# First stage of a fused two-block kernel: the inputs are loaded first, the modulation products run in four column groups with four weight buffers, and the first projection is issued by parts

## The chip, the core and the metric

The kernel is one program on one core of a Trainium2 chip. Its engines each follow their own instruction list and meet only at semaphores: TensorE (PE in the rows, PEld for its weight loads), VectorE (DVE), ScalarE (ACT), GpSimd (POOL) and SyncE (SP), which issues all DMAs of this kernel. The metric is the device time of one execution in microseconds, the median of several runs. Everything the kernel multiplies is float32. Large products are made from three cheaper ones: each operand is split in a rounded part (`_hi`) and a remainder (`_lo`), and hi·hi + hi·lo + lo·hi is accumulated. The small products of the first stage are plain float32 instead, and such a matmul shows in the trace as two records.

## What is computed

Two transformer-like blocks on 256 tokens of width 1024. The change touches only the beginning of the first:

```python
sh1x, sc1x, g1x, sh2x, sc2x, g2x = split(silu(c) @ w_ada + b_ada, 6)      # modulation for x
sh1c, sc1c, ...                  = split(silu(c_ctx) @ w_ada + b_ada, 6)  # and for the context
hc = rms_norm(ctx, norm1_g) * (1 + sc1c) + sh1c
hx = rms_norm(x,   norm1_g) * (1 + sc1x) + sh1x
z  = hx @ w_in      # u, vs, q, r, ga, gb, k, v, lr;  of hc only k, v, lr
```

After that come a spatial gating unit, a two-directional gated linear attention (GLA) with its log-decays from `lr`, a merge, a convolutional FFN, and then the whole second block (gated delta rule, two more FFNs).

## The kernel before

Activations stand transposed: 128 partitions by 8 slices `k` of the width, by tokens. `x` and `ctx` are normalized and modulated side by side, so a slice of `a_parts` (`a_hi`, `a_lo`) has 256 + 256 columns. Weights of the projections stream as units of 512 KB, 128 x 1024 each, through four slots of `w_raw`: SP loads unit u when GpSimd has split unit u-4 (`lo_ready`), ScalarE rounds it to `w_hi` (line 1622) once TensorE has used the slot, GpSimd subtracts to `w_lo` (line 644), TensorE multiplies. Units 0 to 3 are `w_k`, 4 to 7 `w_q`, 8 to 15 `w_v`, 16 to 23 `w_vs`.

The first stage, up to the `w_k` tiles:

- **Modulation rows.** The first 2048 columns of `w_ada` (shift and scale) are in four blocks j of 2 MB, in two buffers `adab`. `mod_rows(j)` on TensorE (line 1000) multiplies `silu(c)`, `silu(c_ctx)` as a stationary operand of 2 columns with 8 slices of 512 columns, into 2 partitions of bank 6 or 7. ScalarE copies them to `modrow`, `flip_rows(j)` (line 1011) transposes them back into columns.
- **Norm.** ScalarE squares each slice, VectorE adds slices 0 to 5 (`sum_squares`, line 2554), `mean_square` (line 1023) adds the rest over partitions on TensorE, ScalarE takes the root, VectorE the reciprocal.
- **Modulated operand.** For each j VectorE normalizes two slices of both inputs (lines 2587, 2588), builds `mod` and `gain`, and forms the full product and its remainder `a_lo` (lines 2601, 2528), ScalarE writes `a_hi`.
- **`w_k` tiles.** `tile_blocks(s, k0, k1)` (line 1033) multiplies slot s with slices k0 to k1; tiles 0 and 1 start with slices 0 to 3, the last two slices of all four tiles come at the end.
- Then `w_q` (line 734), the low-rank `lr` product (line 1061), and `w_v` by blocks (line 1090), which needs units 8 to 11 at once. Beside its second slices go eight small `logits` products (line 1072), each followed by an `Abs` on ScalarE and an add on VectorE, in two banks, so they pace each other.

The other four fifths of `w_ada` (g1, sh2, sc2, g2) are needed only for x and are not done on TensorE: 16 pairs of rows `p` of 1 MB each go through seven buffers (`adaw`, the table `ADA_RING`) and VectorE multiplies and sums them (`modulations`, line 2621, four instructions for each p). SP issues them by `ada_rows(p)` between the units. The order of every engine is written out by hand; a wait of SP holds up all later DMAs.

## Time and profile before

| | us |
|---|---|
| median of 3 runs | 1280.89 (1279.03 to 1281.66) |
| the profiled execution | 1280.58 |
| its span, first to last instruction | 1278.8 |
| around the span | 1.8 |
| TensorE busy in the span | 1248.2 (98%) |
| start of the `w_k` tiles / of `w_q` / of `w_v` on TensorE | 40.2 / 62.8 / 80.5 |
| squares of ctx / of x start on ScalarE (8 take 2.56) | 16.1 / 21.0 |
| mean granted TensorE clock | 0.990 |

The busy time of TensorE in the profile is pipelined: a record lasts from the issue of a matmul to its modelled end and overlaps the next. What an operation costs is read from start to start. Start times are from the span's start.

### The profile page before, as it was taken

The page shows a single profiled execution, that of the slowest core. Times are in us where ns is not written, and L with a number is a line of the kernel's source. Part 1 is how long each engine was busy: PE and PEld are TensorE (multiplying, and loading weights), DVE is VectorE, ACT ScalarE, POOL GpSimd, SP SyncE. Part 2 cuts the span into 40 slices and gives each one's busy share as a digit, 9 for nine tenths or more (in the row PEclk, how much of TensorE's full clock was granted, in tenths as well). Part 3 has the DMA queues.
Part 4 walks back from the last instruction along what each step waited for, and adds up shares of the span by engine and source line. Part 5 has one row for each costly group of instructions (what it writes and reads, how often), then busy time and mean ns, then how long its engine had stood idle before and what let it go on. Part 6 is the DMA issues. An engine that isn't in the chain of part 4 may idle for free.

```text
span 1278.8 us, 26332 instructions
## 1 busy us (share of the span) xinstructions
PE 1248.2 (98%) x9155; PEld 1161.0 (91%) x9155; DVE 726.7 (57%) x1674; ACT 710.6 (56%) x1283; POOL 881.5 (69%) x387
## 2 busy tenths in 40 slices
PE   9999999999999999999899999999999999999997
PEld 3688899999988898899799989999999999999986
DVE  3989861142487773276864256545633766555633
ACT  3656644553666665476532247656755556666743
POOL 0457957578869888965422237888788887888795
PEclk9999999999999999999989999999999999999999
DMA  9986255356646656734312115555566565665562
GB/s 368 403 340 197 83 199 165 118 162 183 184 137 205 192 178 173 211 109 118 113 51 83 51 55 177 181 174 180 155 186 187 174 181 161 187 182 180 157 194 76
DMA packets 66021, 217.71 MB, mean 170 GB/s; under 512 B 9897, under 2 KB 17321, under 8 KB 62609
## 3 DMA queue, kind: packets, MB, share of 16 engines
q1 hardware_dynamic: 65936, 216.56, 53.6%
q8 instruction: 57, 0.93, 0.3%
q14 instruction: 28, 0.22, 0.1%
HBM read 215.48 MB, written 1.05 MB: 169 GB/s over the span
## 4 chain that ended last, share of the span: by engine, by line
PE 51%; issue 24%; POOL 20%; ACT 2%; DVE 2%; POOLq 0%; ACTq 0%; DVEq 0%
POOL w_lo L644 20%; PE bank L734 13%; PE bank L757 10%; PE bank L849 6%; PE bank L1090 5%; PE bank L763 5%; PE bank L858 3%; PE bank L766 2%; PE bank L853 1%; PE bank L1179 1%; DVE cbuf L2934 1%; PE bank L1156 1%; ACT w_hi L1622 0%; PE bank L695 0%; PE bank L700 0%
## 5 line engine op out<-in xcount | busy, mean ns | idle before, releaser
L644 POOL TENSOR_TENSOR w_lo<-w_raw,w_hi 128x1024 fp32r<-128x1024 f32 x340 | 814.0, 2406 | 359.5 <-ACT w_hi L1622 358.6
L1622 ACT ACTIVATE w_hi<-w_raw 128x1024 fp32r<-128x1024 f32 (+1 forms) x372 | 377.9, 1020 | 126.0 <-PE bank L858 42.7
L757 PE MATMUL bank<-a_hi,w_hi 128*128 128x264 f32 (+3 forms) x704 | 200.5, 285 | 0.1
L757 PE MATMUL bank<-a_hi,w_lo 128*128 128x264 f32 (+3 forms) x704 | 200.2, 284 | 0.0
L757 PE MATMUL bank<-a_lo,w_hi 128*128 128x264 f32 (+3 forms) x704 | 199.9, 284 | 0.0
L734 PE MATMUL bank<-a_parts,w_hi 128*128 128x256 f32 x960 | 173.8, 284 | 0.2
L734 PEld LDWEIGHTS bank<-a_parts,w_hi 128*128 128x128 f32 x960 | 149.7, 192 | 1.0 <-ACTq L1879 0.5
L734 PE MATMUL bank<-a_parts,w_lo 128*128 128x256 f32 x480 | 135.8, 283 | 0.0
L757 PEld LDWEIGHTS bank<-a_hi,w_hi 128*128 128x128 f32 x704 | 132.8, 189 | 0.4 <-DVE a_lo L3515 0.3
L757 PEld LDWEIGHTS bank<-a_lo,w_hi 128*128 128x128 f32 x704 | 132.9, 189 | 0.1
L757 PEld LDWEIGHTS bank<-a_hi,w_lo 128*128 128x128 f32 x704 | 132.9, 189 | 0.0
L3589 DVE SCALAR_TENSOR_TENSOR bank<-row_mean,cols,bank 128x260 f32<-128x260 f32 (+3 forms) x112 | 54.6, 488 | 117.2 <-ACT cols L1622 112.8
L734 PEld LDWEIGHTS bank<-a_parts,w_lo 128*128 128x128 f32 x480 | 92.1, 192 | 0.0
L849 PE MATMUL bank<-g_parts,w_hi 128*128 128x512 f32 x308 | 79.1, 397 | 0.7 <-DVEq L3691 0.7
L2934 DVE SCALAR_TENSOR_TENSOR cbuf<-bank,pv,cbuf 128x189 f32<-128x189 f32 (+2 forms) x176 | 65.6, 423 | 16.4 <-ACT cbuf L1622 15.8
L651 POOL TENSOR_TENSOR w_lo<-w_raw,w_hi x32 | 58.0, 1842 | 24.0 <-ACT w_hi L1622 23.2
L734 PE MATMUL bank<-a_hi,w_hi 128*128 128x272 f32 (+1 forms) x240 | 73.6, 307 | 0.0
L734 PE MATMUL bank<-a_hi,w_lo 128*128 128x272 f32 (+1 forms) x240 | 71.6, 298 | 0.0
L734 PE MATMUL bank<-a_lo,w_hi 128*128 128x272 f32 (+1 forms) x240 | 71.5, 298 | 0.0
L763 PE MATMUL bank<-a_parts,w_hi 128*128 128x512 f32 x256 | 64.2, 393 | 1.7 <-DVE cbuf L2934 1.7
L849 PEld LDWEIGHTS bank<-g_parts,w_hi 128*128 128x128 f32 x308 | 55.0, 188 | 11.1 <-DVEq L3691 0.9
L886 PE MATMUL bank<-g_parts,w_hi 128*128 128x260 f32 x352 | 63.9, 284 | 0.7 <-DVEq L3691 0.7
(523 smaller groups left out, 2785.3 us busy)
## 6 DMA issues: line engine op xcount, KB each, us to landing
w_raw<-in_s SPq DMA_DIRECT2D x284, 512.0 KB, 3.6
w_raw<-in_down SPq DMA_DIRECT2D x48, 512.0 KB, 3.6
adaw<-in_w_ada SPq DMA_DIRECT2D x16, 1024.0 KB, 10.3
w_raw<-in_down SPq DMA_DIRECT2D x24, 384.0 KB, 3.2
adab<-in_w_ada_first SPq DMA_DIRECT2D x8, 1024.0 KB, 8.9
ctxt<-in_ctx SPq DMA_DIRECT2D x1, 1024.0 KB, 11.3
x<-in_x SPq DMA_DIRECT2D x1, 1024.0 KB, 15.3
out_h<-h SPq DMA_DIRECT2D x4, 256.0 KB, 2.6
```

What stands on the lines that cost most here:

```text
L644: pool.tensor_tensor(w_lo[:, s], w_raw[:, s], w_hi[:, s].bitcast(F32), ALU.subtract) \
L651: pool.tensor_tensor(w_lo[:, :, ds(k, 1)], w_raw[:, :, ds(k, 1)], w_hi[:, :, ds(k, 1)].bitcast(F32), ALU.subtract) \
L734: ins = mm(banks[s][:, first:n], w_[:, s, k], x_[:, k, first:n], start=(m == 0), stop=(m == 3 * KD - 1))
L757: ins = mm(banks[bank][:, tk], w_[:, s, k], x_[:, k, tk], start=(m == 0), stop=(m == 3 * KD - 1))
L763: mm(banks[bank][:, :].rearrange("p (two n) -> p two n", two=2), w_hi[:, s, k], a_parts[:, :, k, N1:], start=(k == 0), stop=False)
L849: mm(dst[:, :].rearrange("p (two n) -> p two n", two=2), w_hi[:, s, k], g_parts[:, :, kk, first:n], start=(kk == 0), stop=False)
L858: ins = mm(dst[:, 0:N1], w_lo[:, s, k], g_hi[:, kk, first:n], start=False, stop=(kk == KF - 1))
L886: ins = mm(banks[t][:, first:N2], w_[:, s, k], x_[:, k0 + k, first:N2], start=(m == 0), stop=(m == 3 * KF - 1))
L1090: ins = mm(banks[b][:, :].rearrange("p (u m) -> p u m", u=SLOTS), x_[:, k, tk], w_[:, :, k], start=(k == 0 and i == 0), stop=(k == KD - 1 ...
L1622: return nc.scalar.activation(out_, in_, f, **kw)
L2934: v.scalar_tensor_tensor(dst, frm(banks[banks_of(p)[0]][:, 0:n]), pv[:, ds(pair + w, 1)], dst, ALU.mult, ALU.add).then_inc(conv_seq, 1)
L3589: return v.scalar_tensor_tensor(dst, row_mean[:, N2 - dst.shape[-1]:], by, dst, ALU.mult, ALU.add)
```

## The change

- **SP** loads `ctx`, the constants and `x` first, then block 0 of `w_ada`, units 0 to 3, then blocks 1 and 2; block 3 waits only for the squares' buffers (`std_ready`). There are now four buffers `adab`, each in two halves, on the places of the later `adaw` buffers; `ADA_RING` is renumbered accordingly.
- **Norm sums** are made by TensorE alone: `mean_square` has 8 matmuls instead of 3, VectorE's `sum_squares` is gone. x has a bank of its own (5).
- **`mod_rows`**: the stationary operand is `c2_wide`, 32 columns of which 2 are not zero. Slice k goes to partitions 32·(k mod 4) onward, so four slices in a row use four different column groups, and the result is four partial sums. ScalarE copies all 128 partitions, and `flip_rows` is no transpose but a matmul with `row_pick` (128 x 2), which picks and adds the four partials.
- **Order on TensorE**: 24 instead of 16 warming matmuls, both norm sums, then `mod_rows(0)`; `fill` (dummy 128x128 matmuls, 5, 4 and 8) between; the first two slices of every `w_k` tile before `mod_rows(1)` to `(3)` or between them, and the rest by parts of two slices across all four tiles.
- **VectorE** normalizes all of `ctx` while the norm of x is still under way. Of the later rows it does 7, 1, 1, 6 where it did 9, 1, 1, 4 around the same three fixed steps (`w2s`, `lrs`, the log-decay adds).
- **ScalarE** rounds `w2` (`w2s`) after the copies of `w_q` instead of before them.

```diff
-            for j in range(4):
-                if j >= 2:
-                    sp.wait_ge(ada_done, j - 1)
...
+            small(ctxt[:], a["ctx"], ctx_in)
+            small(averages[:], a["averages"], consts_in)
+            small(x[:], a["x"], x_in)
+            small(pv[:], a["pv"], pv_in)
+            ada_blocks(0)
             for s in range(SLOTS):
                 stream_unit("s0", s, s)
+            ada_blocks(1)
+            ada_blocks(2)
+            sp.wait_ge(std_ready, 2)
+            ada_blocks(3)
...
                 for k in range(KD):
                     if k % 4 == 0:
-                        pe.wait_ge(ada_in[j % 2][k // 4], 16 * (j // 2) + 16)
-                    ins = mm(banks[6 + j % 2][0:2, :], c2[:, k], adab[j % 2][:, k], start=(k == 0), stop=(k == KD - 1))
+                        pe.wait_ge(ada_in[j][k // 4], 16)
+                    g = 32 * (k % 4)
+                    ins = mm(banks[6 + j % 2][g:g + 32, :], c2_wide[:, k], adab[j][k // 4][:, k % 4], start=(k < 4), stop=(k >= 4))
...
                 for i in range(4):
-                    ins = nc.tensor.transpose(banks[2 + j % 2][:, 2 * i:2 * i + 2],
-                                              modrow[:, j % 2, i * P:(i + 1) * P], ident[0:2, 0:2])
+                    ins = mm(banks[6 + j % 2][:, 2 * i:2 * i + 2], modrow[:, j % 2, i * P:(i + 1) * P], row_pick[:],
+                             start=True, stop=True)
...
+            mean_square(RMS_CTX)
+            mean_square(RMS_X)
+            fill(5)
             mod_rows(0)
-            mod_rows(1, 5, lambda: mean_square(RMS_CTX))
+            fill(4)
             flip_rows(0)
-            mod_rows(2, 1, lambda: mean_square(RMS_X))
+            fill(8)
+            first_tile(0)
+            first_tile(1)
+            mod_rows(1)
+            first_tile(2)
             flip_rows(1)
+            first_tile(3)
+            mod_rows(2)
+            tile_blocks(0, 2, 4)
+            flip_rows(2)
             mod_rows(3)
-            flip_rows(2)
...
+            tile_blocks(1, 2, 4)
+            flip_rows(3)
+            for s in range(2, SLOTS):
+                tile_blocks(s, 2, 4)
+            for s in range(SLOTS):
+                tile_blocks(s, 4, 6)
+            for s in range(SLOTS):
                 tile_blocks(s, 6, KD).then_inc(unit_used, 1)
```

SP's list between the first `w_ada` blocks and units 10 and 11 decides when those units come. Here `adaw_...` is one pair of rows p, `w_raw` a unit (x2, x4: so many of them), `w_107` or `w_115` the small matrix `w2`. Before, from `w2` on:

```order
L499 DMA w_107<-in_gla_w 16x512 x5
L535 DMA adaw_97<-in_w_ada 128x2048 [waits row_used]
L502 DMA w_raw<-in_s 128x1024 [waits lo_ready] x2
L535 DMA adaw_98<-in_w_ada 128x2048 [waits row_used]
L502 DMA w_raw<-in_s 128x1024 [waits lo_ready] x2
```

and after:

```order
28 L504 DMA w_115<-in_gla_w 16x512 x6
29 L541 DMA adaw_100<-in_w_ada 128x2048
30 L507 DMA w_raw<-in_s 128x1024 x2
31 L541 DMA adaw_101<-in_w_ada 128x2048
32 L507 DMA w_raw<-in_s 128x1024 x2
```

Ahead of `w2` stand seven pairs of rows before and five after, so of the rows two fewer stand in front of units 8 to 11.

VectorE between the last `a_lo` and the log-decays: x4 are the four instructions of one pair of rows, `la` the log-decay adds. Before:

```order
70 L2630 TENSOR_TENSOR w2s<-w_107,w2s 32x1024
71 L2621 SCALAR_TENSOR_TENSOR adaw_92,mod<-adaw_92,bank 128x512 x4
72 L2633 TENSOR_TENSOR lrs<-bank,lrs 32x512
73 L2621 SCALAR_TENSOR_TENSOR adaw_93,mod<-adaw_93,bank 128x512 x4
74 L2638 TENSOR_SCALAR la<-bank,pv 128x512 x8
```

and after:

```order
64 L2627 SCALAR_TENSOR_TENSOR adaw_101,mod<-adaw_101,bank 128x512 x4
65 L2636 TENSOR_TENSOR w2s<-w_115,w2s 32x1024
66 L2627 SCALAR_TENSOR_TENSOR adaw_105,mod<-adaw_105,bank 128x512 x4
67 L2639 TENSOR_TENSOR lrs<-bank,lrs 32x512
68 L2627 SCALAR_TENSOR_TENSOR adaw_106,mod<-adaw_106,bank 128x512 x4
69 L2644 TENSOR_SCALAR la<-bank,pv 128x512 x8
```

The sequence is the same, but `w2s` now stands after 7 pairs of rows instead of 9, and six instead of four pairs follow the `la` adds.

ScalarE at the end of `w_q`, before (`q_79` is a tile's copy out of its bank):

```order
45 L1622 ACTIVATE w2s<-w_107 96x1024
...
53 L1622 ACTIVATE q_79<-bank 128x256
54 L1622 ACTIVATE w_hi<-w_raw 128x1024
...
57 L1622 ACTIVATE lrs<-bank 96x512
58 L1771 ACT_TABLE_LOAD
59 L1622 ACTIVATE ebuf<-bank,pv 128x512 x8
```

and after:

```order
50 L1637 ACTIVATE q_79<-bank 128x256
51 L1637 ACTIVATE w_hi<-w_raw 128x1024
...
54 L1637 ACTIVATE w2s<-w_115 96x1024
55 L1637 ACTIVATE lrs<-bank 96x512
56 L1785 ACT_TABLE_LOAD
57 L1637 ACTIVATE ebuf<-bank,pv 128x512 x8
```

`w2s` moved behind the rounding of unit 11 (the last `w_hi` there); the table load waits, in both kernels, until VectorE has done nine pairs of rows.

## Rows read from the trace of the kernel before

**Rows 1.** The page: busy time, then granted clock in 40 slices.

```profile
PE 1248.2 (98%) x9155; PEld 1161.0 (91%) x9155; DVE 726.7 (57%) x1674; ACT 710.6 (56%) x1283; POOL 881.5 (69%) x387
PEclk9999999999999999999989999999999999999999
```

**Rows 2.** Busy time, clock, DMA share and GB/s by stage, 7 to 80.5 us.

```profile
core 0: us, PE busy (x) PEld busy (x) DVE busy (x) ACT busy (x) POOL busy (x), PEclk, DMA share, GB/s
7.00:18.50 11.50, 10.46 (x24) 1.98 (x24) 1.38 (x4) 2.45 (x8) 0.00 (x0) 1.00 1.01 421
18.50:62.80 44.30, 44.23 (x164) 24.23 (x164) 36.94 (x86) 24.80 (x45) 11.89 (x6) 1.00 1.02 404
62.80:80.50 17.70, 17.35 (x120) 15.33 (x120) 17.64 (x54) 8.46 (x13) 17.61 (x7) 1.00 1.00 388
```

**Rows 3.** TensorE in order of time: start, length, line, operands, count [idle before].

```profile
20.36 1.56 PE L1023 MATMUL bank<-sq,averages 128*128 128x256 f32 x6
21.85 1.88 PE L1000 MATMUL bank<-adab,c 128*2 128x512 f32 x4
32.87 7.03 PE L1000 MATMUL bank<-adab,c 128*2 128x512 f32 x16
62.84 0.51 PE L734 MATMUL bank<-a_parts,w_hi 128*128 128x256 f32 x2
74.45 0.63 PE L1061 MATMUL bank<-a_parts,wlr_hi 128*96 128x512 f32 x2
80.52 0.73 PE L1090 MATMUL bank<-w_hi,a_parts 128*128 128x512 f32 x2 [0.33 <-POOL w_lo L644]
```

**Rows 4.** A later group of small matmuls in several column groups, and the matmul after it.

```profile
605.40 1.08 PE L1329 MATMUL bank<-mt,lane_pick 32*32 32x128 f32 x32
606.40 0.39 PE L734 MATMUL bank<-a_hi,w_hi 128*128 128x272 f32 x1
```

**Rows 5.** ScalarE in order of time: unit 4, `w2s`, units 8 and 10, first `Abs`.

```profile
59.24 1.05 ACT L1622 ACTIVATE w_hi<-w_raw 128x1024 fp32r<-128x1024 f32 x1
65.11 1.06 ACT L1622 ACTIVATE w2s<-w 96x1024 fp32r<-96x1024 f32 x1 [0.52 <-DMA w<-in_gla_w]
68.40 1.06 ACT L1622 ACTIVATE w_hi<-w_raw 128x1024 fp32r<-128x1024 f32 x1 [1.97 <-DMA w_raw<-in_s]
73.47 1.06 ACT L1622 ACTIVATE w_hi<-w_raw 128x1024 fp32r<-128x1024 f32 x1 [1.31 <-DMA w_raw<-in_s]
84.49 0.69 ACT L1622 ACTIVATE ebuf<-bank,pv 128x512 f32<-128x512 f32 x1 [2.37 <-PE bank L1072]
```

**Rows 6.** GpSimd in order of time: units 4 to 11.

```profile
60.37 20.09 POOL L644 TENSOR_TENSOR w_lo<-w_raw,w_hi 128x1024 fp32r<-128x1024 f32 x8 [15.38 <-ACT w_hi L1622]
```

**Rows 7.** VectorE in order of time: two rounds of the operand, `w2s`, `la`, the first scan.

```profile
35.23 0.68 DVE L2587 TENSOR_TENSOR ctxt<-ctxt,bank 128x512 f32<-128x512 f32 x1
40.68 0.68 DVE L2587 TENSOR_TENSOR ctxt<-ctxt,bank 128x512 f32<-128x512 f32 x1
76.65 1.53 DVE L2630 TENSOR_TENSOR w2s<-w,w2s 32x1024 fp32r<-32x1024 f32 x1
78.22 0.69 DVE L2621 SCALAR_TENSOR_TENSOR adaw<-adaw,bank 128x512 f32<-128x512 f32 x1
80.85 0.68 DVE L2633 TENSOR_TENSOR lrs<-bank,lrs 32x512 fp32r<-32x512 f32 x1
103.84 2.34 DVE L2647 SCALAR_TENSOR_TENSOR la<-la,ebuf 128x2048 f32<-128x2048 f32 x1
```

**Rows 8.** GLA stage: what VectorE delivers last, and TensorE's uses of it.

```profile
135.41 1.21 DVE L2682 TENSOR_TENSOR qd<-q,qd 128x1024 f32<-128x1024 f32 x1
140.97 1.09 PE L1145 MATMUL bank<-ident,ks 128*128 128x128 f32 x8
154.41 3.24 DVE L2707 TENSOR_TENSOR ks<-kd,kmul 128x2048 f32<-128x2048 f32 x1
162.41 1.09 PE L1145 MATMUL bank<-ident,ks 128*128 128x128 f32 x8
```

More of the change, by code:

```diff
@@ L160, in bass_two_blocks @@
         la = at("la", [P, 2, HG, 2 * N1], arena + 69632)
-        adab = [at(f"adab{i}", [P, KD, 4 * P], arena + o_) for i, o_ in enumerate((69632, 36864))]
-        modrow = at("modrow", [2, 2, 4 * P], arena + 4096)
-        ADA_RING = [5, 6, 0, 1, 2, 3, 4, 5, 6, 0, 1, 4, 0, 1, 4, 1]
+        adab = [[at(f"adab{i}{half}", [P, KD // 2, 4 * P], o_) for half, o_ in enumerate(two_)] for i, two_ in enumerate(
+            ((arena + 69632, arena + 77824), (arena + 36864, arena + 45056), (arena + 53248, arena + 61440), (area_h, area_s)))]
+        modrow = at("modrow", [P, 2, 4 * P], arena + 4096)
+        c2_wide = at("c2_wide", [P, KD, 32], arena)
+        row_pick = at("row_pick", [P, 2], arena + 1024)
+        ADA_RING = [2, 3, 4, 5, 6, 0, 1, 5, 6, 0, 1, 4, 0, 1, 4, 1]
         adaw = [at(f"adaw{i}", [P, 2, D], o_) for i, o_ in enumerate(
@@ L599, in _ @@
                             small(w2[r0:r0 + RANK, d], a["gla_w2"][d], w2_in)
-                    ada_rows(7)
+                    sp.wait_ge(ada_done, 4)
+                    ada_rows(5)
                     slot_units(8, 10)
-                    ada_rows(8)
+                    ada_rows(6)
                     slot_units(10, 12)
-                    for p in range(9, 12):
+                    for p in range(7, 12):
                         ada_rows(p)
@@ L638, in _ @@
             pool.memset(eps6[:, 1:2], 1e-5).then_inc(fills, 1)
+            pool.memset(c2_wide[:], 0.0).then_inc(fills, 1)
             pool.sem_inc(banks_free, SLOTS)
@@ L987, in _ @@
             pe.wait_ge(warm, 1)
-            for _ in range(16):
+            for _ in range(24):
                 mm(banks[0][:, 0:P], part_sum[:, 0:P], part_sum[:, 0:P], start=True, stop=True)
@@ L1056, in _ @@
             pe.wait_ge(rank_lo, WLR_ROUNDED)
[L1057 removed]
+            pe.wait_ge(mod_taken, 4)
             m = 0
@@ L1710, in modulated @@
                     ins.then_inc(split_hi, 1)
-            mod_rows(0)
             act.wait_ge(x_in, 16)
@@ L1717, in _ @@
             root(RMS_X, N1, 0)
+            mod_rows(0)
+            round_unit(0, 0)
+            round_unit(1, 1)
+            modulated(0)
+            round_unit(2, 2)
+            round_unit(3, 3)
             mod_rows(1)
-            modulated(0)
-            round_unit(0, 0)
-            mod_rows(2)
-            round_unit(1, 1)
             modulated(1)
-            round_unit(2, 2)
-            mod_rows(3)
-            round_unit(3, 3)
-            modulated(2)
-            modulated(3)
+            for j in (2, 3):
+                mod_rows(j)
+                modulated(j)
             act.wait_ge(small_in, 48)
@@ L2545, in normalise @@
                         remainder(i, k - 1, ops, of[:, k - 1:k, first:], shift and shift(k - 1), first)
-            def sum_squares(i, squares):
-                for k in range(1, KD - 2):
-                    dve.wait_ge(sq_ready, 8 * i + k + 1)
-                    if k > 1:
-                        dve.wait_ge(sum_seq, 4 * i + k - 1)
-                    ins = v.tensor_tensor(squares[:, 0], squares[:, 0], squares[:, k], ALU.add)
-                    ins.then_inc(sum_seq if k < KD - 3 else sum_ready, 1)
             def one_over(i, r, c):
@@ L2577, in _ @@
             link(v.memset(qmul[:], 1.0))
-            sum_squares(RMS_X, sqx[:, :, 0:N1])
             one_over(RMS_CTX, r_ctx, rstd[:, N1:2 * N1])
+            for j in range(4):
+                two = slice(2 * j, 2 * j + 2)
+                v.tensor_tensor(ctxt[:, two], ctxt[:, two], lanes(r_ctx, 2), ALU.mult).then_inc(xr_ready, 1)
             one_over(RMS_X, r_x, rstd[:, 0:N1])
@@ L2586, in _ @@
                 two = slice(2 * j, 2 * j + 2)
-                v.tensor_tensor(ctxt[:, two], ctxt[:, two], lanes(r_ctx, 2), ALU.mult).then_inc(xr_ready, 1)
                 v.tensor_tensor(xr[:, two], x[:, two], lanes(r_x, 2), ALU.mult).then_inc(xr_ready, 1)
                 dve.wait_ge(mod_flipped, j + 1)
-                shift_, scale_ = (banks[2 + j % 2][:, 4 * part:4 * part + 4].rearrange("p (k j) -> p k j", j=2) for part in range(2))
+                shift_, scale_ = (banks[6 + j % 2][:, 4 * part:4 * part + 4].rearrange("p (k j) -> p k j", j=2) for part in range(2))
                 v.tensor_tensor(mod[:, :, two].rearrange("p j k -> p k j"), shift_, twice(b_ada[:, 0, two]), ALU.add)
@@ L2616, in modulations @@
                     ring = ADA_RING[p]
-                    dve.wait_ge(row_in[ring], 16 * ADA_RING[:p + 1].count(ring))
+                    dve.wait_ge(row_in[ring], 16 * ADA_RING[:p + 1].count(ring) + 16)
                     for t in range(2):
```

104 lines of the change are left out of this document (42 added, 62 removed).

## The prediction

> **What bounds the kernel now.** First the busy shares: TensorE is busy 98% of the span, no other engine over 69% [rows 1]. So the first question for any edit is which TensorE work or wait it takes away. Then the table by stage, since the edit lies in one stage: from 18.5 to 62.8 us TensorE is busy 44.23 of 44.30 us, at full clock, so the stage up to the end of `w_k` is limited by TensorE's own list [rows 2]. The same table shows a second thing to remember: the DMA engines' share is 1.0 or more in all these rows too, at 388 to 421 GB/s. TensorE is saturated and the DMA stream beside it is also saturated; whatever shortens the first meets the second. Third the order of time on TensorE: `w_q` starts at 62.84, `lr` at 74.45, and `w_v` at 80.52 after 0.33 us of waiting for GpSimd's `w_lo` [rows 3]. GpSimd runs 20.09 us without a gap for units 4 to 11, from 60.37 to 80.46 [rows 6]. So at 80.5 two chains end together: TensorE's (11.6 us `w_q` + 6.1 us `lr`) and GpSimd's (8 units of 2.5 us). A third is close: ScalarE stands idle for unit 8 until 68.40 and for unit 10 until 73.47 because they have not landed [rows 5].
>
> **Part 1, the modulation products on TensorE.** 32 matmuls, 8 of them in 7.03 us [rows 3], that is 0.87 each and 28 us in all. They become 32 matmuls with the same columns in four column groups. No such form (128 rows, 32 columns) is in the trace. The nearest row: 16 plain float32 matmuls of 128 columns (32 records) in four groups of rows and columns start at 605.40, and the next full-width matmul starts at 606.40 [rows 4]. At the rate of the modulation products (0.87 us for 512 columns, 0.22 for 128) they would take 3.5 us one after another; they took 1.0 with the change of form on both sides. So four run beside each other. Those differed in rows as well; the bounds are 7.0 us for a block (no overlap) and 1.75 (four at once). I take 2.0, nearest to the row. TensorE's work falls by 28 − 8 = 20 us.
>
> The Trainium skill ("TensorE: Matmul & The Clock Gate", Part 3) gives 2.38 times for three products of 32 columns in a column packing; an estimate from that page is 2.9 us for a block. By that figure the stage would end about 1 us later and the forecast would not move, because of part 4.
>
> **Part 2, the rest of TensorE's list.** Norm sums: 16 matmuls instead of 6; 3 take 1.49 us from 20.36 to 21.85 [rows 3], so 10 more cost 5.0 us. 17 `fill` and 8 more warming matmuls at about 0.22 are 5.5 us. `w_k` stays: 96 matmuls, 62.5 − 40.2 less one flip = 21.9 us. All `flip_rows` stay near 0.4 us each. These additions lie before 20 us, where the stage waits for data anyway.
>
> **Part 3, when the stage ends.** The stream moved 0.42 MB per us in the first stretch [rows 2]; ctx, the constants and x, 2.4 MB in all, are there at about 10.5 instead of 21.0. Squares on ScalarE to 13, norm sums to 15.7, `mod_rows(0)` to 18.8, copy, flip 20.0. VectorE needs 35.23 to 40.68 = 5.45 us for one j [rows 7], 4.85 without the ctx product that it now does earlier; the first j is done at 24.4. From there the blocks of `w_ada` pace it: by bytes block 1 lands at 26.2, block 2 at 31.3, block 3 at 36.3. Each then costs 2.0 (products) + 0.6 (copy) + 1.4 to 1.7 (a `tile_blocks` part placed ahead of the flip) + 0.4, so the flip of j = 3 is at 40.0. What TensorE has left then is ten parts of two slices, 10 × 1.36 = 13.6 us: the stage ends at 53.6, slot 0 is free at 49.5. Before: 62.6 and, three parts earlier, 58.6. The stage ends **9 us** earlier. With no overlap of the column groups it would have 53 us of work behind 17: 70.5.
>
> **Part 4, what takes over.** From slot 0 free to the start of `w_v` it takes 80.5 − 58.6 = 21.9 us by TensorE and GpSimd, which would give 71.4. But units 10 and 11 must be there. Count the stream in the order of SP's list. Before, ahead of and with unit 8 stand the inputs, all `w_ada` blocks, units 0 to 7, `w2`, eight pairs of rows and unit 8. After, ahead of and with unit 10 stand the same inputs, blocks, units 0 to 7 and `w2`, seven pairs of rows and units 8, 9, 10. One pair less is 1 MB, two units more are 1 MB: the same bytes. In a saturated stream unit 10 therefore lands when unit 8 did, at 68.4 [rows 5]; SP no longer waits for block buffers near 25 us, I give it 0.4: 68.0. Unit 11 follows 0.5 MB later, 69.3. ScalarE 1.05 → 70.4; GpSimd does unit 10 from 69.3 to 71.7 and unit 11 to 74.2. So `w_v` starts at **74.3**, 6.2 us earlier and not 9, and TensorE stands idle from about 71 to 74.
>
> **Part 5, the logits.** ScalarE's table load before the first `Abs` waits for nine pairs of rows. Before, VectorE's ninth was done by 76.6, and the first `Abs` was 3.97 us behind the start of `w_v` (84.49 − 80.52) [rows 3, 5]. Now the chain is: unit 11 rounded 70.4, `w2s` (1.06) 71.5, VectorE's `w2s` (1.53) 73.0, a pair of rows 2.44 (four instructions at 0.61) 75.5, `lrs` 76.2, the ninth pair 78.7, table load 1.28, `Abs` at 80.0. Natural would be 74.3 + 4.0 = 78.3. The eight logits pace each other and TensorE waits in their midst: **1.8 us** is given back. What remains is 6.2 − 1.8 = 4.4 us.
>
> **Part 6, the GLA stage.** Six pairs of rows instead of four stand between the logits and the scans, 4.9 us. VectorE's scans, at 103.84 before [rows 7], start at 103.84 − 4.4 + 4.9 = 104.3; nothing is gained there. TensorE's first use that needs VectorE last: the sixteenth pair is done at 135.41 and the transposes start at 140.97, 5.5 us of slack; for the second direction `ks` is ready at 157.65 and used at 162.41, 4.8 [rows 8]. A lag of 4.9 fits the first and is 0.1 over at the second. I charge nothing; if that cover is gone it costs 1 us. Behind it TensorE's list is shifted as a whole. ScalarE, GpSimd and SP edits otherwise (memset of `c2_wide`, wider copy) are below 0.1 us on any chain.
>
> **Sum.** 1280.58 − 4.4 = 1276.2 in terms of the profiled execution; the median is 0.3 higher: **1276.4**.
>
> **Rivals.** (a) *The column groups do not overlap* (float32 takes two passes, all four share the same rows). For it: only rows-and-columns groups were seen. Against it: 1.0 us where 3.5 would be serial. Then the stage ends at 70.5 instead of 62.6, `w_v` starts 8 us later, the time is 1280.9 + 7.9 = 1288.8: **slower**. It turns slower once a block takes over about 4.5 us. (b) *DMA is not the limit* (the stream runs faster without the early stops): `w_v` at 71.4, gain 9.1, less 1.5 for the logits: 1273.3. For it: the stretch from 62.8 on runs at 388 GB/s, under the 421 of the first one [rows 2]. Against it: the transfers of that stretch stay the same. (c) *More is given back*: TensorE idles 3 us before `w_v`, restarts at half clock (1.2 GHz) and loses up to 1.7; VectorE's lag shows as 1; unit 11 lands 1 us later. Together 3.7: 1280.1. For it: the granted clock does fall in one later slice, to 8 tenths [rows 1]. Against it: the first 1.8 us of such a loss lie behind the logits' wait.
>
> **How the numbers follow.** The sum as worked out (DMA paces, 3 to 6 us gained) 0.56, (b) 0.13, (c) 0.17, (a) 0.10, something else 0.04. The range takes in (b) and (c): 1272.8 to 1280.2. What a measurement of this kernel can tell from no change is about 0.2%, 2.6 us; of (c) most is within, of the sum's case a little: faster 0.74, same 0.13, slower 0.13.
>
> **What would show it.** In the new profile: a block of modulation products in about 2 us (near 7: rival a); `w_q` starting near 54; ScalarE waiting for `w_raw` at unit 10 and 11 near 68 to 69 and TensorE idle before `w_v` on GpSimd's `w_lo`; `w_v` at 74.3 (71.4: rival b); the first `Abs` more than 5 us behind it, after a wait for VectorE's rows; the scans near 104; the first `w_u` tile 4 to 5 us earlier than before, and every later stage by as much. The forecast is wrong if the stage ends after 58, or if the units' landing doesn't follow the count of bytes.

## The result, and the profile after

The change made the kernel **slower**: 1285.37 us in the median of 8 runs (1275.46 to 1287.64), against 1279.67 for the kernel before, measured beside it (8 runs, 1274.25 to 1281.66). The ratio is 1.004, 95% interval 1.0021 to 1.006, that is 2.7 to 7.7 us. The forecast was 1276.4, and 1285.37 is outside its range.

The profiled execution of the new kernel took 1287.6 us with a span of 1285.8, two microseconds more than its median. The first line of the page and its clock row, to be set beside [rows 1]:

```profile
PE 1249.2 (97%) x9241; PEld 1176.8 (92%) x9241; DVE 726.4 (56%) x1665; ACT 711.2 (55%) x1283; POOL 881.6 (69%) x388
PEclk9989999999999999999999999999999999999999
```

TensorE's busy time has hardly changed although 20 us of products went: norm sums, fills and stretches at half clock have filled it up. So busy time tells nothing here. The order of time does. TensorE in the new kernel, from the first stage to `w_v` (start, length, line, operands, count, idle before), the answer to [rows 3]:

```profile
16.63 1.92 PE L1008 MATMUL bank<-adab,c_wide 128*32 128x512 f32 x16
28.42 2.18 PE L1008 MATMUL bank<-adab,c_wide 128*32 128x512 f32 x16
32.03 0.95 PE L1016 MATMUL bank<-row_pick,modrow 128*128 128x2 f32 x8
...
57.38 0.39 PE L740 MATMUL bank<-a_parts,w_hi 128*128 128x256 f32 x1
...
69.00 0.40 PE L1076 MATMUL bank<-a_parts,wlr_hi 128*96 128x512 f32 x1
...
74.57 0.62 PE L1105 MATMUL bank<-w_hi,a_parts 128*128 128x512 f32 x2
```

A block of eight modulation products went from 7.03 us to 1.92, `w_q` starts at 57.38 instead of 62.84, and `w_v` at 74.57 instead of 80.52: **5.95 us earlier**. At `w_v` the change is where the forecast wanted it (74.3). From here on the lead is lost. Below are the last steps of ScalarE before the logits, the answer to [rows 5], and VectorE's between its pairs of rows, the answer to [rows 7]:

```profile
68.38 1.06 ACT L1637 ACTIVATE w_hi<-w_raw 128x1024 fp32r<-128x1024 f32 x1 [1.68 <-DMA w_raw<-in_s]
70.31 1.06 ACT L1637 ACTIVATE w_hi<-w_raw 128x1024 fp32r<-128x1024 f32 x1 [0.60 <-DMA w_raw<-in_s]
71.28 1.04 ACT L1637 ACTIVATE w2s<-w 96x1024 fp32r<-96x1024 f32 x1
74.77 0.60 ACT L1637 ACTIVATE lrs<-bank 96x512 fp32r<-96x512 f32 x1 [2.44 <-PE bank L1076]
81.19 1.28 ACT L1785 ACT_TABLE_LOAD   x1 [5.83 <-DVE adaw L2627]
82.49 1.26 ACT L1637 ACTIVATE ebuf<-bank,pv 128x512 f32<-128x512 f32 x2
```

```profile
72.35 3.00 DVE L2636 TENSOR_TENSOR w2s<-w,w2s 32x1024 fp32r<-32x1024 f32 x1 [2.68 <-ACT w2s L1637]
77.94 0.68 DVE L2639 TENSOR_TENSOR lrs<-bank,lrs 32x512 fp32r<-32x512 f32 x1
92.85 0.75 DVE L2644 TENSOR_SCALAR la<-bank,pv 128x512 f32<-128x512 f32 x1 [0.18 <-ACT ebuf L1637]
110.02 2.29 DVE L2653 SCALAR_TENSOR_TENSOR la<-la,ebuf 128x2048 f32<-128x2048 f32 x1
```

VectorE stands idle 2.68 us for `w2s`, takes 3.00 us for a remainder that took 1.53 before, and ScalarE then waits 5.83 us with its table load for the ninth pair of rows. The scans start at 110.02 instead of 103.84. TensorE waits for the logits, and its clock falls behind that wait. TensorE's waiting row, then two stretches of the table of busy time and granted clock:

```profile
84.02 0.80 PE L1087 MATMUL bank<-lrs,w2s 96*128 96x512 f32 x1 [3.25 <-DVE la L2644]
```

```profile
core 0: us, PE busy (x) PEld busy (x) DVE busy (x) ACT busy (x) POOL busy (x), PEclk, DMA share, GB/s
83.80:90.60 6.80, 6.58 (x16) 5.21 (x17) 3.07 (x5) 2.69 (x4) 0.00 (x0) 0.51 0.34 137
104.00:165.00 61.00, 58.54 (x299) 49.01 (x298) 59.91 (x68) 33.41 (x52) 52.06 (x29) 1.00 0.43 145
```

For 6.8 us the granted clock is 0.51, the lower of the two levels (1.2 GHz). The table of [rows 2] ends at 80.5; the kernel before has 1.00 behind it too:

```profile
80.52:104.00 23.48, 23.48 (x100) 18.36 (x101) 19.96 (x54) 18.68 (x22) 5.09 (x5) 1.00 0.66 250
```

In the GLA stage (the line from 104 to 165 us) VectorE is busy 59.91 of 61 us, against 57.28 before, and it is now the bound of the stage. TensorE waits for it three times, the answer to [rows 8], where it did not wait at all:

```profile
142.55 1.06 PE L1160 MATMUL bank<-ident,ks 128*128 128x128 f32 x8 [1.03 <-DVE adaw L2627]
162.05 1.13 PE L1141 MATMUL bank<-qd,ki 128*128 128x128 f32 x8 [1.43 <-DVE kd L2709]
168.13 1.18 PE L1160 MATMUL bank<-ident,ks 128*128 128x128 f32 x8 [2.65 <-DVE st L2728]
```

The last row is the second key transposes, 5.72 us later than in [rows 8]. Behind that wait come another 3.4 us at half clock (0.51 from 168.90 to 172.30), and the first matmul of the GLA outputs starts at 226.44 where it started at 219.25. These 7.19 us then stay (6.99 at the end):

```profile
226.44 0.39 PE L1194 MATMUL bank<-qs,st 128*128 128x128 f32 x2
```

### The profile page after: what moved, and what is told of

Read it like the earlier page. It is cut to its first block, busy times and chain, and to the rows that moved or that the text cites. A ratio compares the mean times of both kernels' runs of the same rounds, so it can differ in the third digit from the quotient of the medians.

```text
span 1285.8 us, 26487 instructions
## 1 busy us (share of the span) xinstructions
PE 1249.2 (97%) x9241; PEld 1176.8 (92%) x9241; DVE 726.4 (56%) x1665; ACT 711.2 (55%) x1283; POOL 881.6 (69%) x388
## 4 chain that ended last, share of the span: by engine, by line
PE 45%; issue 24%; POOL 19%; DVE 7%; ACT 2%; DMA 1%; POOLq 0%; ACTq 0%; DVEq 0%
POOL w_lo L650 19%; PE bank L740 13%; PE bank L763 10%; PE bank L855 6%; PE bank L769 5%; PE bank L864 3%; PE bank L772 2%; DVE adaw L2627 1%; PE bank L859 1%; DVE ebuf L2658 1%; PE bank L1194 1%; DVE cbuf L2940 1%; DVE kd L2709 1%; ACT w_hi L1637 0%; DMA w_raw<-in_s 0%
```

## The experiments

In short, the theory to be tested: *what decides the time is when VectorE gets to the scans and what stands between them and `st`, not when the first stage ends*. Its rivals, by place: the logits, the transfers, the weights. For each kernel the table gives four places of one profiled execution (VectorE's scans, the second key transposes on TensorE, the first matmul of the GLA outputs and its distance from before) and the median of its runs less the median of before measured beside it. Between 560 and 770 us short stretches at half clock occur in all kernels, before included (mean granted clock 0.93 to 0.97 there in the executions profiled), so the whole time of a single execution is a worse witness than the outputs column, and a difference of medians has an interval of about 2 us either way.

The first two columns vary as well. Up to its scans e12 is the same program as after, and e6 differs only in the order of the products inside a modulation block; their scans are at 105.31 and 108.82, where after's profiled execution has 110.02. So a scan time of one execution can differ by some 5 us with no edit behind it. The distance from the scans to the second keys is steadier, and the arguments on the GLA stage below rest on it.

| kernel | scans | second keys | outputs | against before | median against before | ratio (95%) |
|---|---|---|---|---|---|---|
| before | 103.84 | 162.41 | 219.25 | | | |
| after | 110.02 | 168.13 | 226.44 | +7.19 | +5.7 | 1.004 (1.0021 to 1.006) |
| e1_w2s_early | 104.80 | 162.92 | 222.44 | +3.19 | +2.9 | 1.0018 (1.0001 to 1.0035) |
| e2_ring | 105.32 | 163.44 | 221.74 | +2.49 | +1.2 | 1.0012 (0.9998 to 1.0025) |
| e3_both | 103.66 | 161.67 | 219.83 | +0.58 | +0.3 | 0.9996 (0.9983 to 1.0009) |
| e4_before_split | 115.70 | 174.07 | 232.17 | +12.92 | +10.0 | 1.0066 (1.0046 to 1.0087) |
| e7_before_lag | 107.39 | 165.36 | 222.17 | +2.92 | +4.9 | 1.0041 (1.0026 to 1.0057) |
| e8_memset_last | 104.00 | 160.87 | 217.67 | -1.58 | -0.4 | 0.9995 (0.9976 to 1.0014) |
| e5_two_pairs_less | 101.11 | 160.28 | 218.63 | -0.62 | -0.2 | 1.0005 (0.9987 to 1.0023) |
| e9_pool | 102.53 | 159.29 | 216.09 | -3.16 | -1.9 | 0.999 (0.997 to 1.001) |
| e12_after_reordered | 105.31 | 160.05 | 216.85 | -2.40 | -2.9 | 0.9981 (0.9959 to 1.0002) |
| e11_before_reordered | 103.57 | 162.13 | 218.96 | -0.29 | -0.4 | 0.9997 (0.9979 to 1.0015) |
| e10_queries_last | 103.24 | 157.62 | 214.41 | -4.84 | -6.7 | 0.995 (0.9929 to 0.9971) |
| e6_pairs | 108.82 | 166.54 | 224.89 | +5.64 | +4.4 | 1.0028 (1.0007 to 1.0049) |

### The logits stage

**e1_w2s_early**: after, with ScalarE's `w2s` ahead of the `w_q` copies, where before has it.

```diff
-            lin("w_q", lambda t, s: fn(q1[:, ds(t, 1)], ...
             act.wait_ge(w2_in, 96)
             fn(w2s[:], w2[:], ACT.Copy).then_inc(rank_hi, 1)
+            lin("w_q", lambda t, s: fn(q1[:, ds(t, 1)], ...
```

> The changed kernel with one part undone: ScalarE rounds w2 (w2s) before the copies of w_q, as in the kernel before. In the changed kernel w2s is at 71.28, VectorE's remainder of it ends at 75.35, the ninth pair of rows at 81.1 and the first Abs starts at 82.49. Theory A (the logits are late because the ninth pair hangs behind w2s): VectorE's remainder moves to about 70, the ninth pair ends at 78 to 79, the first Abs is near 80, TensorE's wait before the third logits product falls from 3.25 to about 1 us, and the scans start 2 to 3 us earlier than 110.0; the time falls by 2 to 4 us, to a ratio of about 1.001 to the kernel before. Rival B (the pairs of rows themselves come too late by DMA): the ninth pair stays at 81, the first Abs at 82.5, the time within 1 us of the changed kernel.

ScalarE rounds `w2` at 59.02; VectorE no longer waits for it, the first `Abs` starts at 80.10 instead of 82.49, the half clock at 83.8 is gone and the scans start 5.2 us earlier. How much of this is the edit's is not shown: e12, without it, has its first `Abs` at 80.04, no half clock there and its scans at 105.31, and the intervals of the medians (after 2.7 to 7.7, e1 0.1 to 4.5) overlap. The table load still waits:

```profile
69.66 3.31 DVE L2636 TENSOR_TENSOR w2s<-w,w2s 32x1024 fp32r<-32x1024 f32 x1
78.81 1.28 ACT L1785 ACT_TABLE_LOAD   x1 [3.52 <-DVE adaw L2627]
```

**e2_ring**: after, with row pairs 7 and 8 in buffers 2 and 3 instead of 5 and 6. The logits' `ebuf` lies on the latter, so the table load and the first `Abs` then wait for five pairs instead of nine.

```diff
-        ADA_RING = [2, 3, 4, 5, 6, 0, 1, 5, 6, 0, 1, 4, 0, 1, 4, 1]
+        ADA_RING = [2, 3, 4, 5, 6, 0, 1, 2, 3, 0, 1, 4, 0, 1, 4, 1]
...
-            act.wait_ge(row_used, 9)
+            act.wait_ge(row_used, 5)
```

> The changed kernel with another place for two pairs of rows: pairs 7 and 8 use buffers 2 and 3, which ScalarE's ebuf doesn't cover, so that ScalarE's table load waits for five pairs instead of nine. w2s stays late. Theory A: the first Abs follows the first logits product (about 79.5 instead of 82.5), VectorE's first la add follows the ninth pair at 81.2 instead of 83.2, TensorE's wait falls from 3.25 to about 1.3 us: 2 us gained, time 2 us below the changed kernel. Rival B (DMA): VectorE waits for the rows and nothing moves by over 0.5 us. Rival C (the loss is one of the clock alone): the clock still falls to half near 84 and the scans stay at 110.

The table load has no wait any more (74.93). The first `Abs`, at 80.42, now waits for TensorE, which in this execution started `w_v` only at 76.44, after waiting 2.15 us for GpSimd's `w_lo`. The 4.7 us by which the scans are earlier than in after's execution are again no more than e12 shows without the edit; for it speaks the median, 1.2 us above before against 5.7.

**e3_both**: the two together.

> The changed kernel with w2s early and pairs 7 and 8 in buffers 2 and 3. Theory A: the logits follow w_v almost without a wait (under 0.7 us), no half clock near 84, la adds end near 88 instead of 93.6, the scans start at 104 to 105 instead of 110.0 and TensorE's waits in the GLA stage (1.0, 1.4, 2.7 us) shrink to 0 to 2 us together; unit 12 is 5 us and unit 60 4 to 6 us ahead of the kernel before: ratio 0.996 to 0.998. Rival D (the six pairs ahead of the scans bind whatever the logits do): unit 12 is ahead by 5 us, but unit 60 is within 1.5 us of the kernel before or behind it.

The first `Abs` is at 79.04. `w_v` starts 5.45 us earlier than before (75.07), and the first unit that GpSimd splits behind the logits also starts 5.45 us earlier (91.39 against 96.84): the lead of the first stage has come through the logits whole. Yet the scans, with two more pairs of rows ahead of them, are only 0.18 us earlier, and the outputs start 0.58 us *later* than before. So the logits are not the only place where the lead is lost; VectorE's list behind them takes back 6 us by itself. The median agrees: 0.3 us above before (interval -2.2 to +1.2), clear of after's. TensorE's rows in the GLA stage look as in after, only 6.5 us earlier:

```profile
136.08 1.06 PE L1160 MATMUL bank<-ident,ks 128*128 128x128 f32 x8 [0.49 <-DVE adaw L2627]
155.58 1.13 PE L1141 MATMUL bank<-qd,ki 128*128 128x128 f32 x8 [1.44 <-DVE kd L2709]
161.67 1.94 PE L1160 MATMUL bank<-ident,ks 128*128 128x128 f32 x8 [2.66 <-DVE st L2728]
```

**e4_before_split**: the kernel before, with only the two edits of order: `w2s` behind the `w_q` copies, and VectorE's pairs 7, 1, 1, 6.

```diff
-            modulations(0, 9)
+            modulations(0, 7)
...
-            modulations(11, 15)
+            modulations(9, 15)
```

> The kernel before with two parts of the change alone: w2s after the copies of w_q, and VectorE's pairs of rows split 7, 1, 1, 6 instead of 9, 1, 1, 4 around w2s, lrs and the la adds. The first stage, the DMA order and the column groups are those of before. Theory A plus D: the first Abs waits for the ninth pair (w2s near 76, ninth pair near 83, Abs near 85 to 86 instead of 84.5), the scans start 5 to 6 us later, near 109.5, and TensorE waits in the GLA stage; the time rises by 2 to 5 us, ratio 1.002 to 1.004. Rival E (the harm comes from the new first stage: stream, clock, column groups): the time stays within 1 us of before.

Without the new first stage the same order costs 12.9 us at the outputs and 10.0 in the median. VectorE idles 5.22 us for `w2s`, and the table load waits 5.52 for its ninth pair. After is 5.7 us ahead of this kernel at the outputs, and 4.3 in the median: that is the worth of the new first stage, near the 5.95 seen at `w_v`.

```profile
77.13 3.54 DVE L2630 TENSOR_TENSOR w2s<-w,w2s 32x1024 fp32r<-32x1024 f32 x1 [5.22 <-ACT w2s L1622]
86.51 1.28 ACT L1771 ACT_TABLE_LOAD   x1 [5.52 <-DVE adaw L2621]
174.07 1.94 PE L1145 MATMUL bank<-ident,ks 128*128 128x128 f32 x8 [2.65 <-DVE st L2722]
```

In the table, after and these four have one thing in common: the second keys start 58.0 to 58.4 us behind the scans, wherever the scans are. Before, not waiting, has 58.6. So its slack was about 0.6 us. The next two runs test this from both sides.

### The slack of the GLA stage

**e7_before_lag**: the kernel before, with VectorE held up right ahead of the scans by three repeated memsets.

```diff
+            for _ in range(3):
+                link(v.memset(sc_full[0][:], 0.0))
             decays(0)
```

> The kernel before with three more memsets of the zeroed score tile (1024 elements a partition, 0.91 us each where the trace of before has one at the same size) on VectorE right ahead of the first `la` scan step; nothing else is changed. It prices a lag of VectorE of 2.7 us at the scans, which start at 103.84 us in before. Theory A (the wait that binds is TensorE's for the second state `st`, with 0.6 us of slack): scans at 106.6, the second direction's key transposes at 106.6 + 58.0 = 164.6 instead of 162.4, and everything after it some 2.1 us later; the time 1281.5 to 1282. Theory B (the forecast's: slack of 4.8 us at the second keys): scans at 106.6, second keys still at 162.4, time as before, 1279.9.

The three memsets, each awaited, held it up by 3.55 us rather than 2.7. The second keys came 2.95 later, so 0.60 was slack, and the outputs 2.92 later. The forecast's slack of 4.8 us would have swallowed all of it. The median rose by more, 4.9 us (3.3 to 7.3); the profiled execution is the fastest of the twelve, and what the others lost beyond 2.9 us no trace shows. The waiting row has the same name as in after:

```profile
165.36 1.06 PE L1145 MATMUL bank<-ident,ks 128*128 128x128 f32 x8 [2.66 <-DVE st L2724]
```

In before VectorE itself stands idle in this stage, 0.53 and 0.80 us for score products, 1.15 for `kd` and 0.49 ahead of `st`; in e7 these waits are gone, yet its way from the scans to the end of `st` takes 57.8 us instead of 57.0. The idle time was no cover, because steps got longer when they ran at another moment: the first `kd` product 3.38 instead of 2.28 us, the second `qd` 2.33 instead of 1.21, the last two `kmul` products together 2.39 instead of 0.38.

**e8_memset_last**: e3, and on VectorE the memset of the second score tile behind `second_state(0)`.

```diff
-            link(v.memset(sc_full[1], 0.0))
             second_state(0)
+            link(v.memset(sc_full[1], 0.0))
```

> The kernel after with both repairs of the logits stage (w2's parts ahead of the w_q copies on ScalarE, and row pairs 7 and 8 on buffers 2 and 3), and on VectorE the memset of the second score tile (0.91 us) behind `second_state(0)` instead of ahead of it. Theory A (TensorE waits for `st`): second keys 0.95 us earlier than in the same kernel without the move (161.67 with scans at 103.66), so 57.05 us after the scans instead of 58.0; time about 0.9 us less than that kernel's 1280.2. Theory B (TensorE waits for `ks`, or has slack there): second keys stay 58.0 us after the scans and the time stays.

The second keys are 56.87 us behind the scans instead of 58.0, and the wait for `st` is 1.45 instead of 2.66: what stands ahead of `st` on VectorE counts one for one. No half-clock stretch follows the wait; the outputs start 2.16 us earlier than in e3.

**e12_after_reordered**: after, with nothing but this memset and the decayed queries (`qs` of the second direction, 2.25 us) moved behind `second_state(0)`. First stage, pairs and logits are those of after.

```diff
             def chunk_factors(d):
...
-                v.tensor_tensor(by_chunk(qs[d]), by_chunk(qd[d]), ...)
+                if not d:
+                    decayed_queries(0)
...
-            link(v.memset(sc_full[1], 0.0))
             second_state(0)
+            decayed_queries(1)
+            link(v.memset(sc_full[1], 0.0))
```

> The kernel after, its first stage and its logits stage untouched; on VectorE, in the second direction of the GLA stage, the decayed queries (2.25 us) and the memset of the second score tile (0.91 us) stand behind `second_state(0)` instead of ahead of it. Theory A (VectorE's `kd` and `st` in this place are what turns the late scans into a late TensorE): scans still at 110.0, the second keys 3.16 us nearer to them, at 110.0 + 54.9 = 164.9 instead of 168.13, no wait for `kd` (1.43 in after) or under 0.3, a wait for `st` of some 1; GpSimd's units from 185 us on 3.2 to 5 us earlier than in after (up to 1.7 of it a half-clock stretch near 168.9 that goes), so +2.2 to +4 against before instead of +7.19; time 1281 to 1283. Theory B (something else late by 6 us holds them, the projections of w_v or GpSimd): +7.2 stays, time 1285.

The second keys are 54.7 us behind the scans (54.9 worked out), the wait for `kd` is gone and that for `st` is 0.65:

```profile
157.63 1.16 PE L1141 MATMUL bank<-qd,ki 128*128 128x128 f32 x8
160.05 1.06 PE L1160 MATMUL bank<-ident,ks 128*128 128x128 f32 x8 [0.65 <-DVE st L2732]
```

The median is 1277.87, 2.9 us below before (interval -5.2 to +0.3) where after is 5.7 above: **the order of two VectorE steps takes away the whole loss.** Whether this kernel is faster than before its interval leaves open. e6, which differs from after only inside the modulation blocks, was measured beside it and has 1285.12, 7.3 us more. Part of the distance in the profile is not the edit's: the scans of this execution start at 105.31, 4.7 us earlier than in after's, with the same program up to there. Of the 8.6 us between the two differences from before 3.2 to 5 were worked out ahead; the intervals (about 2.6 us each way) can hold the rest, and no run here tells more.

**e11_before_reordered**: the same two steps moved in the kernel before.

> The same move of the two VectorE steps in the kernel before, and nothing else. Theory A (slack of 0.6 us at `st` in before, TensorE not waiting there): second keys at 162.4 as in before, units from 185 us on within 0.3 us of before, time 1279 to 1280. If the keys come more than 0.5 us earlier, TensorE does wait there in before, and the slack of 0.6 us is wrong.

Scans and second keys are both 0.3 us earlier than in before, the outputs too, the median 0.4: nothing. TensorE does not wait there in before. What VectorE saved went into its own waits: 3.48 us for `kd` (1.15 before) and 2.48 for TensorE ahead of `st` (0.49 before). The step order was harmless in before and decisive in after.

### What stands ahead of the scans

**e5_two_pairs_less**: e3, with VectorE's products of row pairs 9 and 10 left out (their eight modulation columns are set to zero; all transfers stay).

```diff
                     dve.wait_ge(row_in[ring], ...)
+                    if p in (9, 10):
+                        v.memset(mod[:, :, 16 + 2 * p:18 + 2 * p], 0.0).then_inc(row_used, 1)
+                        continue
```

> The kernel after with both repairs of the logits stage, and the products of row pairs 9 and 10 left out on VectorE (their eight modulation columns are set to zero, their DMAs still run): this takes two pairs of 2.45 us, 4.9 us, out of VectorE's work ahead of the scans. Theory A (VectorE's lag is what TensorE waits for in the GLA stage): scans at 98.8 to 99.5 instead of 103.66, all of TensorE's waits there gone (1.44 for `kd`, 2.66 for `st`), no half clock near 161 us, the offset from before on GpSimd's units from 185 us on goes from +0.6 to -4 or -5, time 1274.5 to 1276. Theory B (TensorE's own work or the weights bound the stage): the scans move, the second keys and the units after them don't, time 1280.

Neither theory's number held. Of the 4.9 us taken out, the scans gained 2.55, since VectorE then waits for the rows themselves. The second keys gained only 1.39 and are 59.17 us behind the scans, not 58.0: the first step of the scans (last row) takes 3.25 us where e3's takes 2.29. The median is 0.2 us below before, within the noise.

```profile
93.37 0.69 DVE L2630 SCALAR_TENSOR_TENSOR adaw<-adaw,bank 128x512 f32<-128x512 f32 x1 [2.48 <-DMA adaw<-in_w_ada]
96.21 0.69 DVE L2630 SCALAR_TENSOR_TENSOR adaw<-adaw,bank 128x512 f32<-128x512 f32 x1 [0.33 <-DMA adaw<-in_w_ada]
101.11 3.25 DVE L2656 SCALAR_TENSOR_TENSOR la<-la,ebuf 128x2048 f32<-128x2048 f32 x1
```

**e9_pool**: e8, with `w2`'s remainder and the memset of the first score tile given to GpSimd, which has nothing to do from about 75 us on.

```diff
             remainders(0, GROUP0)
+            pool.wait_ge(rank_hi, W2_ROUNDED)
+            pool.tensor_tensor(w2s[last_rows], w2[last_rows], w2s[last_rows].bitcast(F32), ALU.subtract)...
+            pool.memset(sc_full[0][:], 0.0).then_inc(pool_done, 1)
```

> The kernel of the memset's move, with two more things taken from VectorE ahead of the scans and given to GpSimd, which is idle from 75 to 84 us: w2's remainder (3.38 us on VectorE there) and the memset of the first score tile (0.91). Theory A (VectorE's sum ahead of the scans is late by what the edit added): scans 3.5 to 4.3 us earlier than 103.66, at 99.4 to 100.2, second keys at 157 to 158, units from 185 us on 4 to 5 us earlier than with the memset's move alone; time 1275 to 1276.5, under both kernels. Theory B (rows 12 to 15, which SP issues last, are what VectorE then waits for): scans no earlier than 102.5, with waits on the rows' DMA of 2 us or more in place of the work that went, time 1279.

On the scans the second theory was right: 102.53, only 1.5 us earlier than e8's for 4.2 us of work taken away (3.31 and 0.91). VectorE waits 2.48 us twice for rows (at 66.82 and 71.82) instead. Below is GpSimd, then VectorE:

```profile
74.09 2.39 POOL L657 TENSOR_TENSOR w2s<-w,w2s 32x1024 fp32r<-32x1024 f32 x1
```

```profile
66.82 0.69 DVE L2635 SCALAR_TENSOR_TENSOR adaw<-adaw,bank 128x512 f32<-128x512 f32 x1 [2.48 <-DMA adaw<-in_w_ada]
71.82 0.69 DVE L2635 SCALAR_TENSOR_TENSOR adaw<-adaw,bank 128x512 f32<-128x512 f32 x1 [2.48 <-DMA adaw<-in_w_ada]
```

**e10_queries_last**: e9 with the decayed queries moved as in e12.

> The kernel with both repairs of the logits stage, the work given to GpSimd and the memset's move, and now also the decayed queries of the second direction behind `second_state(0)`. Theory A: the scans stay at 102.5, TensorE's waits for `kd` (1.43) and `st` (1.45) go, the second keys start at 156.5 to 157.1 instead of 159.29, units from 185 us on another 2.2 us earlier; time about 1275, faster than before by 0.3%. Theory B (the layer norm's sums, 2.25 us later by the move, or the scores are then what TensorE waits for): keys earlier, but units from 185 us on are not; time 1277.

This is the best kernel: 1274.06 us (9 runs), ratio 0.995 to before (0.9929 to 0.9971), faster than both. The wait for `kd` is gone and `st` costs 0.67. The outputs start 4.84 us earlier than before; in this execution `w_v` starts at 74.41, 6.11 us earlier, so four fifths of the lead are kept.

```profile
157.62 1.06 PE L1168 MATMUL bank<-ident,ks 128*128 128x128 f32 x8 [0.67 <-DVE st L2738]
214.41 0.39 PE L1202 MATMUL bank<-qs,st 128*128 128x128 f32 x2
```

### The column groups

**e6_pairs**: after, with the slices of a modulation block in the order 0, 4, 1, 5, 2, 6, 3, 7, so that two products in a row use the same column group.

```diff
-                for k in range(KD):
-                    if k % 4 == 0:
-                        pe.wait_ge(ada_in[j][k // 4], 16)
+                pe.wait_ge(ada_in[j][0], 16)
+                pe.wait_ge(ada_in[j][1], 16)
+                for k in (0, 4, 1, 5, 2, 6, 3, 7):
```

> The kernel after, with the eight products of each modulation block in the order 0, 4, 1, 5, 2, 6, 3, 7, so that two products in a row stand in the same column group. It prices the overlap of the column groups by itself. Forecast's part 1 (groups run beside each other when neighbours lie in different ones): a block of eight goes from 1.92 us to 3.5 to 4, the first stage's end some 5 to 7 us later less what waits for DMA there, w_v's start (74.57) by less than 1 us later since the weights' transfers set it; time as after, 1285. Rival: blocks stay at 1.92 us, so neighbours need not alternate. Second rival (a late first stage moves the later transfers by its own slot releases): w_v 3 us or more later, and time 1288.

The rival was right: a block still takes 1.94 us, and the next matmul starts 1.88 behind it.

```profile
27.87 1.94 PE L1008 MATMUL bank<-adab,c_wide 128*32 128x512 f32 x16
29.75 0.74 PE L1034 MATMUL bank<-a_parts,w_hi 128*128 128x512 f32 x2
```

So neighbours need not lie in different groups, and this run prices no lost overlap. What makes a product of 0.87 us one of 0.24 stays open between overlap of groups over more than two neighbours and something else in the new form.

## Where the forecast was right and where not

**Part 1 (modulation products): right.** 2.0 us a block was taken, 1.92 measured (2.18 where the half clock touches it). The Trainium skill ("TensorE: Matmul & The Clock Gate", Part 3) has 2.38 times for three products of 32 columns in a column packing; this trace has 7.03 / 1.92 = 3.7 times with four groups, so the estimate of 2.9 us from it was too high and the measurement decides.

**Parts 2 and 3 (the end of the first stage): too early by 3.8 us, almost without effect.** `w_q` starts at 57.38, not 53.6. The forecast's own terms give 40.7 for the last flip (36.3 + 2.0 + 0.6 + 1.4 + 0.4), not 40.0, and 70.0, not 70.5, for the case without overlap. Each `flip_rows` takes 0.8 to 0.9 us from start to start, not 0.4; block 1's products run only at 28.42, after the tiles put ahead of them; 3.4 us near 25.6 are at half clock. The forecast called itself wrong "if the stage ends after 58"; it was close to that.

**Part 4 (transfers take over): right, also in its size.** By the count of bytes units 10 and 11 were to be there at 68.0 and 69.3: ScalarE waits for them until 68.38 and 70.31. `w_v` was to start at 74.3: 74.57. The idle time of 3 us that was to stand ahead of it is not there: TensorE is busy 17.19 of the 17.19 us from `w_q` to `w_v`, because `w_q` came later than forecast, and GpSimd's last `w_lo` is ready at 74.28. The two chains end together. In other executions of the same first stage `w_v` starts between 73.83 and 76.44 (e6, e2), with up to 2.15 us of waiting for `w_lo`.

**Part 5 (logits): right mechanism, term too small.** The first `Abs` was forecast for 80.0 and came at 82.49. Each link of the chain slipped: `w2s` starts at 71.28 instead of 70.4, VectorE's remainder takes 3.00 us instead of 1.53. And it was not the end of it: behind TensorE's wait of 3.25 us stood 6.8 us at half clock, so the `la` adds end at 93.6, later than in before, instead of 1.8 us of 6.2 being lost. The wrong terms are the price of VectorE's step, taken from one row of before, and the half clock, put at nothing in the sum. How much they were worth can be read against e12, the same program up to the scans: there the step takes 1.32 us, no half clock follows, and the scans are 4.7 us earlier.

**Part 6 (GLA stage): the step that failed.** The forecast said that VectorE's lag "fits the first and is 0.1 over at the second" and charged nothing, with the slack read between `ks` ready (157.65) and used (162.41). But the second keys also wait for `st`, the second state, and this stands on VectorE *behind* `ks` and a memset. The kernel before, VectorE, in the rows that follow the `ks` of [rows 8]:

```profile
157.81 0.91 DVE L2746 MEMSET spare_lo<- 128x1024 f32 x1 [0.16 <-issue]
159.21 1.66 DVE L2722 SCALAR_TENSOR_TENSOR st<-st,bdec,bank 128x256 f32<-128x256 f32 x4 [0.49 <-PE bank L1160]
```

VectorE's last delivery for TensorE was ready at 160.87, not 157.65, which leaves 1.54 us to 162.41 and not 4.8; and measured by e7 a lag at the scans had 0.60 us of slack. By that alone the sum falls: scans at 104.3, as forecast, give second keys at 104.3 + 58.0 = 162.3, where before has 162.41. That is no gain at all, 4.4 us less than forecast. The scans' further 5.7 us (110.02 against 104.3) are 5.7 us of loss, and the half clock behind the `st` wait adds 1.5. Together 0 + 5.7 + 1.5 = 7.2 us at the outputs, which is what the trace shows. Had only the slack been read rightly, the forecast would have been "no change", 1280.8; e3, whose logits behave as the forecast wanted or better, indeed measured 1280.16.

**The rivals.** (a) did not happen, (b) neither. (c), "more is given back", had the right sign of the error and VectorE's lag among its causes, but priced the lag at 1 us; it was worth 4.4 us with the scans where they were forecast, and 10 where they were. Its half clock was to follow an idle time ahead of `w_v`; it came, but behind the logits' wait (the granted clock is 0.99 from 74.57 to 83.80). Its unit 11 did land 1 us later than forecast, and moved `w_v` by no more than 0.3. Only (a) had a slower kernel, and for a reason that did not occur; no case that let the groups overlap had the sign. The range ended at "all given back", while the edits of order alone cost more than the new first stage brings (e4: 12.9 us).

## What to carry to other kernels

Slack is read at the consumer: list every semaphore that the waiting instruction tests, and take the producer that comes last in its engine's order, not the one that has the nearest name. When work is moved on an engine that is busy over 90% of a stage, assume that its lag arrives whole, and look for steps ahead of the awaited one that nobody needs yet; moving two of them (3.2 us of work) took away the whole loss of 5.7 us. Idle time of the lagging engine is no cover by itself: in e7 2.97 us of it went and the delivery still came later by more than the lag. And an edit that starts a stage earlier should leave the order of the stages behind it alone until it has been measured by itself.

## What the runs showed of the hardware

**One VectorE step, 1.3 to 3.5 us, by who starts first.** `w2`'s remainder (32x1024, two operands in SBUF) took 1.53 us in before, 3.00 in after, 3.31 in e1, 3.38 in e3, 3.54 in e4, 3.30 in e6, and 1.33 in e2 and 1.32 in e12. GpSimd makes remainders of 2.4 us at the same time, also from two operands. In e3 GpSimd had started one at 69.28 and was busy until 71.69; VectorE's step, started at 69.39, ended at 72.77, 1.08 later. In e12 VectorE started first, and GpSimd's group of two that began at 69.41 took 5.72 us instead of 4.78:

```profile
69.28 2.41 POOL L650 TENSOR_TENSOR w_lo<-w_raw,w_hi 128x1024 fp32r<-128x1024 f32 x1 [0.41 <-ACT w_hi L1637]
```

```profile
71.58 1.32 DVE L2636 TENSOR_TENSOR w2s<-w,w2s 32x1024 fp32r<-32x1024 f32 x1 [2.06 <-ACT w2s L1637]
```

```profile
69.41 5.72 POOL L650 TENSOR_TENSOR w_lo<-w_raw,w_hi 128x1024 fp32r<-128x1024 f32 x2 [0.28 <-ACT w_hi L1637]
```

In these rows whichever starts second waits out the other. The Trainium skill ("SBUF — State Buffer", section "SBUF: two separate sides") has this as an exclusive lock on a port pair for a VectorE operation with two SBUF inputs; the rows agree. It is one part of why the same program has its scans at 105.3 in one execution (e12) and at 110.0 in another (after): 1.7 us are the step's length, 0.8 its later start, and some 2.5 come with the half clock beside the `la` adds. Which engine starts first turns on tenths of a microsecond: in e12 VectorE's step starts at 71.58, in after at 72.35, and GpSimd's next unit is due near 71.9 in both. One of after's eight runs took 1275.46; that it was such a case is a guess. Tiny steps have two prices too: in e10 a product of 8 elements that reads its second operand from a bank takes 0.17 us, and 1.15 where that operand (`dec`) is in SBUF. GpSimd is at work at both times:

```profile
124.23 0.17 DVE L2707 TENSOR_TENSOR bdec<-qmul,bank 128x8 f32<-128x8 f32 x1
145.63 1.15 DVE L2707 TENSOR_TENSOR bdec<-qmul,dec 128x8 f32<-128x8 f32 x1
```

Two `kmul` products of 4 elements, all in SBUF, take 0.38 us in before and 2.39 in e7. That this is the same waiting fits, but no run here separates it from other causes.

**A wait of TensorE costs more than its length.** In after, waits of 3.25 us (at 84.02) and 2.65 us (at 168.13) are followed by stretches of 6.8 and 3.4 us at the lower clock, while e8's wait of 1.45 at the second place is followed by none; there the outputs come 2.16 us earlier than in e3 for a step of 0.9. In e6 a wait of 3.25 us at the first place brought 3.4 us at the lower clock instead of 6.8, and e7's wait of 2.66 brought none, so such a wait does not always have the same price.
